# Rounding the first activation tiles before the output weights in the layer-end stage of a three-layer network

## The reference, cut to what matters

```python
    return (o * jax.nn.silu(z)) @ w_out + b_out          # end of layer 1
...
    return o.astype(h.dtype) @ w_out                     # end of layer 2
...
        x = x + rmsnorm(y, post_norm_w[layer])           # layers 1 and 2
...
    merged = jnp.concatenate([gla_out, rwkv_out], axis=-1).astype(x.dtype)
    return x + merged @ w_out                            # layer 3, then _rmsnorm(x, final_norm_w)
```

## Time and profile before

| what | value |
|---|---|
| time of three executions | 4197.79, 4200.08, 4201.01 us, median 4200.08 |
| the profiled execution | 4198.82 us, of which the span of the instructions is 4197.5 us |
| busy in the span | PE 3830.7 us (91%), DVE 2019.6 (48%), ACT 1521.5 (36%), POOL 985.8 (23%) |
| TensorE clock granted, mean | 0.962 of full |
| layer end 1 | about 774.7 to 1003 us of the span |
| layer end 2 | about 2213.4 to 2440 us |
| layer end 3 | about 3990.0 to 4197.5 us |

### The profile page before, as it was taken

How to read it: one execution, slowest core, us unless ns; L and a number is a source line. 1 busy time by engine, 2 the same in 40 slices (tenths; PEclk the granted TensorE clock), 3 DMA queues, 4 the chain that set the end, 5 groups by cost and what they waited for, 6 DMA issues and landing times.

```text
span 4197.5 us, 73047 instructions
## 1 busy us (share of the span) xinstructions
PE 3830.7 (91%) x30496; PEld 2853.2 (68%) x30496; DVE 2019.6 (48%) x4533; ACT 1521.5 (36%) x2905; POOL 985.8 (23%) x1018
## 2 busy tenths in 40 slices
PE   7999979896999998999997969999999979999989
PEld 4565558685877877878776857776777754655567
DVE  4665552354555555555553346666665651222222
ACT  3444441222444444444443334444444321122132
POOL 0000001232444443444432232322222200000032
PEclk9999989998999999999998989999999989999889
DMA  3000000222101101010103321111111120010032
GB/s 120 22 1 1 1 16 26 85 86 72 36 26 32 30 27 30 25 36 26 31 11 125 131 86 40 37 43 37 38 42 37 38 95 22 0 31 1 0 116 90
DMA packets 186549, 183.36 MB, mean 44 GB/s; under 512 B 6496, under 2 KB 158320, under 8 KB 186224
## 3 DMA queue, kind: packets, MB, share of 16 engines
q1 hardware_dynamic: 186224, 178.69, 13.4%
HBM read 145.12 MB, written 33.55 MB: 43 GB/s over the span
## 4 chain that ended last, share of the span: by engine, by line
PE 80%; DVE 9%; ACT 6%; issue 2%; DMA 2%; POOL 1%; SPq 0%; ACTq 0%; DVEq 0%; POOLq 0%
PE bank L193 15%; PE bank L195 14%; PE bank L194 14%; PE bank L1598 6%; PE bank L1169 4%; PE bank L447 4%; ACT arena L187 3%; PE bank L1655 3%; PE bank L2071 2%; DVE arena L685 1%; PE bank L2082 1%; ACT L277 1%; DVE arena L178 1%; PE bank L487 1%; PE bank L1698 1%
## 5 line engine op out<-in xcount | busy, mean ns | idle before, releaser
L194 PE MATMUL bank<-hT_cut,arena_cut 128*128 128x512 f32 x1824 | 725.3, 398 | 0.0
L187 ACT ACTIVATE arena<-bank 128x512 f32<-128x512 f32 (+1 forms) x584 | 313.0, 569 | 970.9 <-PE bank L195 450.8
L187 ACT ACTIVATE arena<-arena 128x512 f32<-128x512 f32 (+3 forms) x690 | 359.3, 549 | 283.8 <-POOL arena L1352 221.3
L193 PE MATMUL bank<-hT_cut,arena_cut 128*128 128x512 f32 x920 | 424.7, 462 | 8.9 <-DVE hT_cut L1409 8.9
L194 PEld LDWEIGHTS bank<-hT_cut,arena_cut 128*128 128x128 f32 x1824 | 351.2, 193 | 68.3 <-issue 15.2
L188 ACT ACTIVATE arena<-arena 128x256 f32<-128x256 f32 (+2 forms) x336 | 210.1, 626 | 511.6 <-DVE arena L177 276.6
L195 PE MATMUL bank<-hT_cut,arena_cut 128*128 128x512 f32 x920 | 366.5, 398 | 0.0
L193 PE MATMUL bank<-arena_cut,hT_cut 128*128 128x512 f32 x768 | 308.5, 402 | 61.4 <-POOL oT_cut L949 61.4
L2340 POOL TENSOR_TENSOR arena_cut<-arena,arena_cut 128x256 fp32r<-128x256 f32 x272 | 224.0, 854 | 477.6 <-ACT arena_cut L187 477.6
L193 PE MATMUL bank<-oT_cut,arena_cut 128*128 128x512 f32 x648 | 289.4, 447 | 44.3 <-POOL arena_cut L2340 23.0
L194 PE MATMUL bank<-arena_cut,hT_cut 128*128 128x512 f32 x768 | 305.8, 398 | 0.0
(11 more groups left out here) (222 smaller groups left out, 7244.2 us busy)
## 6 DMA issues: line engine op xcount, KB each, us to landing
arena<-in_w_in SPq DMA_DIRECT2D x72, 512.0 KB, 3.8
arena<-in_rec_w_in SPq DMA_DIRECT2D x64, 512.0 KB, 4.1
x_after<-arena SPq DMA_DIRECT2D x32, 512.0 KB, 2.6
arena<-x_after SPq DMA_DIRECT2D x32, 512.0 KB, 4.1
oT<-in_x SPq DMA_DIRECT2D x16, 512.0 KB, 3.6
arena<-in_x SPq DMA_DIRECT2D x16, 512.0 KB, 3.6
h_after<-hT SPq DMA_DIRECT2D x4, 2048.0 KB, 7.7
hT<-h_after SPq DMA_DIRECT2D x4, 2048.0 KB, 16.8
```

The costliest lines, as they stand in the source:

```text
L187: return e.activation(out, a, f, bias=bias, scale=scale)
L193: pe.matmul(out, a[0], b[0], start=start, stop=False)
L194: pe.matmul(out, a[0], b[1], start=False, stop=False)
```

## The change

The calls `cut(0)` and `cut(1)` leave `in_turn`. On ScalarE they now stand ahead of the loop that rounds the weights; on GpSimd they stand right ahead of `in_turn`. The other engines gave `in_turn` an empty `cut`, and lose nothing.

```diff
     def in_turn(cut, first, rest):
-        cut(0)
-        cut(1)
         for t in range(NT):
             if t + 2 < NT:
                 cut(t + 2)
...
+        cut(0)
+        cut(1)
         for c in range(KC):
             a.wait_ge(*w_got[c].by("in"))
             act(a, wo_hi[:, c, :], wo[:, c, :], ACT.Copy).then_inc(*w_a.did("hi"))
...
+        cut(0)
+        cut(1)
         in_turn(cut, nothing, rest)
```

## The result

The changed kernel takes 4170.21 us at the median of six runs (4164.47 to 4174.30), the kernel before 4198.80 us at the median of six. The ratio is 0.9932, with a 95% interval of 0.9919 to 0.9945: about 28.6 us less, where 27.7 less and 4172.4 us had been forecast.

What follows compares the result with a forecast made beforehand. TensorE's waits for GpSimd's activation tiles, queued behind the weights' rounding, bound the three layer-end starts; gains of 9.5, 8.8 and 9.4 us sum to 27.7, giving 4171.1 profiled and 4172.4 median, range 4169 to 4176 (4168 to 4180 with the port rival).

Steps and rivals of the forecast that it cites:

- The place: First product of each of three layer ends: TensorE waits there for GpSimd's lo parts, together 61.4 us.
- The sum: 25th matmul of layer ends 1, 2, 3 comes 9.5, 8.8 and 9.4 us earlier, sum 27.7 us.
- The last piece ends at 789.93, as now: Layer end 1: VectorE's last weight subtraction ends unchanged; its first starts 0.9 us late, regained over seven intervals.
- a sign of being wrong: The prediction would be wrong if VectorE's last piece comes over 1 us late, or PEclk is 0.5 in half 1.
- GpSimd against VectorE: Start of each layer end: VectorE's first weight piece waits for GpSimd's tile 1, 0.9 us late, nothing at the end.
- The first rival: Last weight piece falls behind GpSimd's tile 2: layer end 1 gains 6.0 instead of 9.5; all three, 4182.7 us; chance 0.10.
- The clock: Half 0 of tile 0: TensorE's clock rises while it waits for weights; twelve half-clock matmuls had cost 2.3 us in the open.
- The rival that it stays at half: TensorE's clock stays at half behind half 0 as long as before: gain 19.0, time 4181 us; chance 0.05.
- What is late next: Behind half 1: tile 0's normalization, 3.1 us ahead of its transposes, moves with TensorE, so the gain arrives whole.
- 3 us of the runs' spread: Whole-kernel time: allowance for variation between runs, included in the forecast's own range of 4169 to 4176.

Runs made afterwards that it cites:

- the second pair: Both kernels unchanged, profiled and timed again: the kernel before 4196.66 us (ratio 0.9998), the changed kernel 4168.52 us (0.9928).
- both halves for each piece: Changed kernel, but TensorE works both halves of tile 0 for each weight piece before the next: 4167.84 us, ratio 0.9932.
- the kernel with one tile: Changed kernel, but only tile 0 is rounded ahead of the weights, tile 1 behind them: 4168.91 us, ratio 0.9935.
- the forced case: Changed kernel, but ScalarE rounds tile 2 ahead of the last weight piece, so GpSimd takes it before VectorE has that piece: 4181.87 us, ratio 0.9964.
- the control: Changed kernel, tile 2 rounded ahead of the last weight piece, but GpSimd waits with it until VectorE's last piece is done: 4171.87 us, ratio 0.9941.
- the fillers: Changed kernel with both halves of tile 0 per piece, and matmuls into an unused bank ahead: 64 took 4186.38 us (0.9974), 24 took 4158.76 us (0.9910).

## Why the prediction was right

**The place.** It was read from one row, 61.4 us of TensorE's wait in three events, and all of them are gone.

**The sum.** 9.5, 8.8 and 9.4 us were forecast; measured were 9.2, 8.0 and 9.5 in the first pair of profiles and 9.1, 9.0 and 9.5 in the second. "The last piece ends at 789.93, as now" assumed that the weights land as before. In layer end 1 that end is 15.15 us behind the first issue, in layer end 2 it was 15.0; in the changed kernel it was 15.6 and 15.9. The chain of layer end 1 has the transfer at 9.90 us instead of 9.37 there, and not VectorE. The 0.9 us of layer end 2 are close to the 1 us that the prediction named as a sign of being wrong, but they are the landing too: ScalarE began on the last piece 13.54 us behind the first issue instead of 12.68, and in the second pair it was 12.89 against 13.21. What the mechanism has to answer for, from that point to the 25th matmul, was forecast at 3.25 us (787.62 to 790.87) and measured at 3.17 or 3.18 in all six.

That the median came within 1 us of the forecast is in part luck. The ratio's interval is 5 us wide to either side, the sum of the layer ends was 26.7 and 27.6, and the rest of the 28.6 comes out of phases in which nothing was edited: the recurrence, which took 1.7 us more in both pairs, and the phases behind it, which took 8.3 and 4.4 us less (and 3.9 more in the profile with both halves for each piece).

**GpSimd against VectorE.** The first piece was drawn out by 1.0 us in layer ends 1 and 2 (0.9 forecast) and by 0.3 in 3, VectorE caught up by the last, and it cost nothing. So engines do not meet at semaphores alone, as is said at the start of this document: these two also waited for each other's instructions. That the wait costs nothing is shown by the kernel with one tile: none of its 24 pieces is drawn out, and its sum is the same. The first rival was real as a mechanism and was forced: its price was put at 3.5 us for a layer end by timing alone, and the forced case, which began its wait later, lost 1.4 to 1.6 us to the wait, 0.65 to ScalarE's own rounding, and 1.3 to 1.6 more to the clock in two of three. In the changed kernel GpSimd takes tile 2 when the last piece is under way, as worked out.

**The clock.** That TensorE would leave its half clock while it waits for weights carried 2.3 us of layer end 1's 9.2, and it did, after 4.7 us. The rival that it stays at half did not come; the forced wait shows that it was nearer than the 0.05 given to it made it seem, since 2.35 us of idling sufficed.

**What is late next.** Nothing: 181.66 us behind the 25th matmul of layer end 3, in both kernels.

**What was not foreseen.** The phases that nobody edited differ by up to 10 us from one profile to another, roughly with their clock. "3 us of the runs' spread" was too small for a single profile, which showed 34.4 us, and about right for the median.

## What to carry to other kernels

Ask of each preparation on a slow-starting path which of its inputs arrives last, and put everything that doesn't need that input ahead of it in its engine's queue: the step leaves the chain, and, worth more here (19 of 27 us), its consumer can then work in step with the arrivals. Once a consumer is paced by arrivals, it has idle time that other work can fill, and a clock that can be kept up or raised before the work comes, if the filler ends before the work is there. Judge a change by the stretch that it touches, in two profiles at least, since the rest of the program doesn't hold still.

## What the runs showed of the hardware

The same 16480 matmuls of the delta-rule phase took 989.6 to 999.9 us over fourteen profiles, with 50.9 to 74.0 us at half clock, with VectorE's busy time between 599.5 and 601.6 us, ScalarE's between 414.1 and 414.4, and GpSimd's between 266.9 and 268.0. TensorE's clock fell behind an idle time of 2.35 us between pieces, in two of three places, while waits of 0.3 us between pieces, of 0.8 to 0.9 us before the last one (the control) and of 1.5 us between the fillers and the first piece did not lower it. And a subtraction of VectorE that takes 1.23 us took 2.19 and 2.25 us when it began inside one of GpSimd's (2.64 in the forced case), at the beginning of its row of pieces without a cost, at the end of it with one.
